# One core, a whole transformer in one launch: both row blocks' norms first, high parts first, and attention products for two heads at a time

## The chip, the cores and the metric

The kernel runs on one core of a Trainium2 chip. Its time is device microseconds, from the first to the last instruction and what lies around them. Engines are TensorE (PE), VectorE (DVE), ScalarE (ACT), GpSimd (POOL) and SyncE (SP), each with an instruction stream of its own that runs in order; semaphores tie them together. Smaller is better.

## The reference, cut to what matters

256 rows of width 1024 pass through seven residual stages, each behind an RMS norm, all in 32-bit floats:

```python
h = h + moba_nsa_mixer(rmsnorm(h, mix_norm[0]), ...)   # "even": 8 full-attention heads, 8 with three gated branches
h = h + sqrelu_mlp(rmsnorm(h, mlp_norm[0]), ...)       # mlp0
h = h + fox_mixer(rmsnorm(h, mix_norm[1]), ...)        # "fox": 16 heads, forget gates
h = h + sqrelu_mlp(rmsnorm(h, mlp_norm[1]), ...)       # mlp1
n = modulate(rmsnorm_2(rmsnorm(h, final_norm), g_ffn1), sh1, sc1); h = h + 0.5 * gt1 * swiglu(n, ...)   # norm gf1, glu0
n = modulate(rmsnorm_2(h, g_mix), sh2, sc2);   h = h + gt2 * hybrid_mixer(n, ...)   # norm gmix, "dil": 8 heads
n = modulate(rmsnorm_2(h, g_ffn2), sh3, sc3);  h = h + 0.5 * gt3 * swiglu(n, ...)   # norm gf2, glu1
out = rmsnorm_2(h, g_final)
```

In the even mixer's second half a head's output is `g0 * o_cmp + g1 * o_slc + g2 * o_win` with `g = sigmoid(...)`, and each `o` is a softmax times values.

## The kernel before

**Products in three parts.** Weights stream in as 173 units of 1 MB through a ring of four buffers `raw`. ACT rounds each to a high part `w_hi`, DVE writes the rest to `w_lo` over `raw`. The rows are split in the same way into `a_hi` and `a_lo`. Each product is three matmuls, high times low, low times high, high times high (`three`, L1532 to L1534). A unit is used when `unit_used` counts it, and SP then loads the unit four further on.

**The rows.** There are two blocks of 128 rows, t = 0 and t = 1. Before each stage a block is normed (`squares`, `root` on ACT, `inverse_root` on DVE), scaled into `tok`, turned on PE by eight transposes (`turn_rows`, L1630, in four chunks of two), rounded by ACT (`turned`, L746, or L748 and L753 where a shift is added: gf1, gmix and gf2) and its low part made by DVE (L1167, or L1154 and L1163). Chunk c of block t is announced by `act_high` and then `act_split`.

**Passages.** A passage is the stretch between two stages. `begin_hidden` (before mlp0, mlp1, glu0, glu1) and `begin_values` (before the values of fox and dil) take the products of block 0, and put the turning of block 1 after three quarters of them:

```python
first_rows(name, u, 1, 0, 0)
turn_rows(name, 1)
first_rows(name, u, 1, 0, 1)
```

Each group of products waits for `act_split`, the last part to be made. The first stage's start is written out by hand in the same manner.

**Mixers.** A mixer walks a list of ticks, written by `plan` from estimated lengths. A tick is a half or a quarter of a weight unit's matmuls, and before them come scores of a head (`tick.s`, L1699 and L1700), turning of probabilities (`tick.t`, L1708) and values times probabilities (`tick.pv`, `products`, L1726). A head goes from PE to DVE (bias and minimum, L1226), ACT (exponential, L827), DVE (reciprocal of the sum, L1244 to L1247), POOL (scaling, L565), PE (turn), and ACT or DVE for even or odd heads (copy into one of six `probT`), and back to PE. `products` treats two heads side by side on 64 columns each of the array; `plan` puts them into a tick when two such pairs are turned. `tick.closed` lists output tiles, which are taken from PSUM one tick later (L838, L1253). The even mixer has a small softmax over compressed keys beside the heads: DVE shifts it in tick km0 2, ACT takes exponentials, DVE weighs it in tick km0 3, and PE turns it in the ticks of `CT_AT`.

## Time and profile before

| what | value |
|---|---|
| median of 3 runs | 1103.0 us (1101.99 to 1103.15) |
| the profiled execution: its time, its span | 1100.71 us, 1098.9 us |
| PE busy | 1075.3 us (98%), 6102 matmuls |
| DVE, ACT, POOL busy | 779.2 us (71%), 662.0 us (60%), 112.8 us (10%) |
| granted PE clock in all 40 slices | 9 (0.9 or more of 2.4 GHz) |
| HBM read | 236.15 MB, 216 GB/s over the span |

PE is in work nearly all the time, so the span is its matmuls one after the other, what lies ahead of the first and behind the last of them, and its waits. "Busy" runs from the start of a matmul to its modelled end, and starts of neighbours lie closer together than that; so the distance between starts is what a matmul costs.

### The profile page before, as it was taken

How to read it: one execution, taken by the hardware profiler on the slowest of the kernel's cores; microseconds unless marked ns; L12 is line 12 of the kernel's file. 1: busy time of each engine (PE TensorE's matmuls, PEld its weight loads, DVE VectorE, ACT ScalarE, POOL GpSimd, SP SyncE). 2: the span in 40 equal slices, each digit the busy share in tenths (PEclk: the TensorE clock that was granted, in tenths of full speed). 3: DMA queues.
4: the chain of work that ended last, by engine and by line, in shares of the span. 5: the costliest groups of instructions: out<-in, count | busy, mean ns of one | idle time of the engine just before them, and what ended most of it. 6: DMA issues, size and time to landing. Idle time of an engine off the chain costs nothing.

```text
span 1098.9 us, 15922 instructions
## 1 busy us (share of the span) xinstructions
PE 1075.3 (98%) x6102; PEld 915.4 (83%) x6102; DVE 779.2 (71%) x1272; ACT 662.0 (60%) x1071; POOL 112.8 (10%) x209
## 2 busy tenths in 40 slices
PE   8999999999999999999999999999999999999997
PEld 7988788888888997888888788888878977888885
DVE  6667667877777776676766778887875766565566
ACT  6667677565576776766565764354475766444443
POOL 1032201010100531020000000101000100000000
PEclk9999999999999999999999999999999999999999
DMA  8842348878764632687778457768545445555551
...
DMA packets 40620, 238.31 MB, mean 217 GB/s; under 512 B 4661, under 2 KB 5845, under 8 KB 17632
## 3 DMA queue, kind: packets, MB, share of 16 engines
...
q8 instruction: 49, 0.80, 0.3%
q10 hardware_dynamic: 720, 0.62, 0.2%
q14 instruction: 27, 0.22, 0.1%
HBM read 236.15 MB, written 1.11 MB: 216 GB/s over the span
## 4 chain that ended last, share of the span: by engine, by line
PE 80%; DVE 9%; ACT 6%; issue 3%; DMA 1%; DVEq 0%; SPq 0%; ACTq 0%
PE bank L1563 21%; PE bank L1532 15%; PE bank L1534 14%; PE bank L1533 14%; PE bank L1564 10%; DVE w_lo L1061 2%; PE bank L1726 1%; PE bank L1708 1%; DMA raw<-in_stream 1%; DVE ada_raw L1296 1%; DVE w_lo L1050 1%; ACT w_hi L683 1%; ACT w_hi L694 1%; PE bank L1700 1%; ACT tok L705 1%
## 5 line engine op out<-in xcount | busy, mean ns | idle before, releaser
L1563 PE MATMUL bank<-a_two,w_hi 128*128 128x512 f32 x1088 | 386.9, 399 | 0.8 <-DVE w_lo L1061 0.8
L1061 DVE TENSOR_TENSOR w_lo<-raw,w_hi 128x2048 fp32r<-128x2048 f32 x122 | 278.5, 2303 | 105.3 <-ACT w_hi L694 105.3
L1564 PE MATMUL bank<-a_two,w_lo 128*128 128x256 f32 x1088 | 305.3, 281 | 0.0
L694 ACT ACTIVATE w_hi<-raw 128x2048 fp32r<-128x2048 f32 x122 | 232.2, 1910 | 63.0 <-DMA raw<-in_stream 62.9
L1563 PEld LDWEIGHTS bank<-a_two,w_hi 128*128 128x128 f32 x1088 | 204.4, 188 | 51.1 <-issue 1.3
L1564 PEld LDWEIGHTS bank<-a_two,w_lo 128*128 128x128 f32 x1088 | 205.5, 189 | 1.7
L1532 PE MATMUL bank<-w_lo,hid_hi 128*128 128x512 f32 x432 | 169.5, 392 | 0.1
L1533 PE MATMUL bank<-w_hi,hid_lo 128*128 128x512 f32 x432 | 168.6, 390 | 0.0
L1534 PE MATMUL bank<-w_hi,hid_hi 128*128 128x512 f32 x432 | 168.4, 390 | 0.0
L866 ACT ACTIVATE cross<-bank 128x256 f32<-128x256 f32 x136 | 51.5, 381 | 187.0 <-PE bank L1564 186.6
L1050 DVE TENSOR_TENSOR w_lo<-raw,w_hi 128x1024 fp32r<-128x1024 f32 x104 | 125.4, 1224 | 25.5 <-ACT w_hi L683 25.0
L683 ACT ACTIVATE w_hi<-raw 128x1024 fp32r<-128x1024 f32 x104 | 106.5, 1050 | 21.2 <-DMA raw<-in_stream 20.9
L1532 PEld LDWEIGHTS bank<-w_lo,hid_hi 128*128 128x128 f32 x432 | 81.1, 188 | 18.9 <-DVE hid_lo L1268 1.0
L1534 PEld LDWEIGHTS bank<-w_hi,hid_hi 128*128 128x128 f32 x432 | 81.1, 188 | 17.8
L1533 PEld LDWEIGHTS bank<-w_hi,hid_lo 128*128 128x128 f32 x432 | 81.1, 188 | 15.2
L1532 PE MATMUL bank<-a_two,w_hi 128*128 128x256 f32 x320 | 93.5, 292 | 0.0
L1534 PE MATMUL bank<-a_two,w_hi 128*128 128x256 f32 x320 | 90.4, 283 | 0.0
L1533 PE MATMUL bank<-a_two,w_lo 128*128 128x256 f32 x320 | 90.4, 282 | 0.0
L1296 DVE CUSTOM_DVE_ANT_0 ada_raw<-ada_raw,silu_row 128x1024 f32<-128x1024 f32 x72 | 84.8, 1219 | 5.2 <-DMA ada_raw<-in_ada 3.5
L1261 DVE TENSOR_TENSOR hid_act<-bank,cross 128x256 f32<-128x256 f32 x96 | 39.1, 420 | 56.5 <-ACT cross L866 56.5
L580 POOL DMA_DIRECT2D ada_raw<-in_ada x72 | 38.1, 530 | 325.9 <-DVE modc L1296 325.9
L1532 PE MATMUL bank<-w_lo,a_two 128*128 128x512 f32 (+1 forms) x160 | 62.1, 388 | 6.1 <-DVE a_two L1167 3.0
...
## 6 DMA issues: line engine op xcount, KB each, us to landing
raw<-in_stream SPq DMA_DIRECT2D x173, 1024.0 KB, 4.9
...
```

The source lines that it names most:

```text
L683: nc.scalar.activation(w_hi[:, u % RING, part_], raw[:, u % RING, part_], ACT.Copy).then_inc(hi_ready, 1)
L694: nc.scalar.activation(w_hi[:, u % RING, :], raw[:, u % RING, :], ACT.Copy).then_inc(hi_ready, 2)
L866: nc.scalar.activation(cross[:, slot, nt, :], ps[bank][:, T:2 * T], ACT.Copy).then_inc(done, 1)
L1050: nc.vector.tensor_tensor(w_lo[:, u % RING, part_], raw[:, u % RING, part_], w_hi[:, u % RING, part_].bitcast(F32), ALU.subtract).then_inc ...
L1061: nc.vector.tensor_tensor(w_lo[:, u % RING, :], raw[:, u % RING, :], w_hi[:, u % RING, :].bitcast(F32), ALU.subtract).then_inc(lo_ready, 2)
L1261: nc.vector.tensor_tensor(to[:, nt * T:(nt + 1) * T], ps[bank][:, 0:T], cross[:, slot, nt, :], ALU.add).then_inc(done, 1)
L1296: nc.vector.tensor_tensor_reduce(part, part, silu_row[:, :], 1.0, 0.0, ALU.mult, ALU.add, modc[:, p:p + 1]).then_inc(ada_done, 1)
L1532: nc.tensor.matmul(dst, l_hi, r_lo, start=start, stop=False)
L1533: nc.tensor.matmul(dst, l_lo, r_hi, start=False, stop=False)
L1534: return nc.tensor.matmul(dst, l_hi, r_hi, start=False, stop=stop)
L1563: nc.tensor.matmul(ps[bank][:, 0:2 * T], wh[:, k, cols_], a_two[:, :, k, :], start=k == 0, stop=False)
L1564: ins = nc.tensor.matmul(ps[bank][:, T:2 * T], wl[:, k, cols_], a_hi[:, k, :], start=False, stop=k == KT - 1)
```

## The change

Five things change.

1. **Start.** The input is loaded in four quarters, on SP's and ACT's queues in turn; half of unit 0 and the table `rpick` move to ACT's queue. DVE squares a half of block 0. Both blocks are normed and scaled before the first weights are split. PE's first products are written out term by term ("h": high times high, "r": high times low weights, "l": low rows), each with its own wait. There are 19 warm-up matmuls where there were 22.
2. **Passages.** `first_rows` and the new `opening` put the products with high rows ahead of those with low rows, and wait for `act_high` and `act_split` apart. Block 1 is turned in two pieces, chunks 0 and 1 an eighth of block 0's products later than before, chunks 2 and 3 another eighth later. DVE's shifts for chunks 1 and 3 no longer come together.
3. **Mixers.** `plan` takes a pair of heads as soon as it is turned, so values times probabilities come for two heads at one time (24 places of one pair, where there were 12 of two). Output tiles are closed one at a tick.
4. **Gates.** The sigmoid is now finished once, in `gates`. DVE's product ahead of each gated head's reciprocal goes, and POOL multiplies by the gate as its second scalar.
5. **Compressed softmax.** Its shift moves to tick km0 3, its exponential to km1 0, its weighing to km1 1, and the first two of its turnings one tick on.

```diff
@@ -43,7 +43,7 @@
-WARM = 22
+WARM = 19
@@ -119,9 +119,9 @@
-            if len(turned) >= 2 and turned[1][0] + lag_pv <= begin:
-                tick.pv += [turned.pop(0)[1], turned.pop(0)[1]]
-                now += 1.3
+            if turned and turned[0][0] + lag_pv <= begin:
+                tick.pv.append(turned.pop(0)[1])
+                now += 0.75
@@ -133,6 +133,9 @@
+    for tick, later, last in reversed(list(zip(ticks, ticks[1:], ticks[2:]))):
+        if len(tick.closed) == 2:
+            later.closed = [tick.closed.pop()] + later.closed
@@ -157,7 +160,7 @@
-CT_AT = [("km1", 0, 1), ("km1", 0, 2), ("qm1", 0, 0), ("qm1", 0, 1)]
+CT_AT = [("km1", 0, 2), ("km1", 0, 3), ("qm1", 0, 0), ("qm1", 0, 1)]
@@ -517,11 +521,9 @@
         def _(sp):
-            sp.dma_start(h[:, 0, :], x[0:P, :]).then_inc(x_landed[0], 16)
-            for part in range(2):
-                part_ = slice(HALF * part, HALF * part + HALF)
-                sp.dma_start(raw[:, 0, part_], stream[0][:, part_]).then_inc(first_landed[part], 16)
-            sp.dma_start(h[:, 1, :], x[P:T, :]).then_inc(x_landed[1], 16)
+            sp.dma_start(h[:, 0, 0:512], x[0:P, 0:512]).then_inc(x_landed[0][0], 16)
+            sp.dma_start(h[:, 1, 0:512], x[P:T, 0:512]).then_inc(x_landed[1][0], 16)
+            sp.dma_start(raw[:, 0, 0:HALF], stream[0][:, 0:HALF]).then_inc(first_landed[0], 16)
@@ -562,7 +564,8 @@
-                        ins = pool.tensor_scalar(p_, p_, wgt[:, 2 * i + t:2 * i + t + 1], 1.0, ALU.mult, ALU.mult)
+                        gate = 1.0 if heads[i][5] is None else gates[:, t, heads[i][5]:heads[i][5] + 1]
+                        ins = pool.tensor_scalar(p_, p_, wgt[:, 2 * i + t:2 * i + t + 1], gate, ALU.mult, ALU.mult)
...
             def mask(c):
@@ -908,22 +910,32 @@
+            act.dma_start(h[:, 0, 512:D], x[0:P, 512:D]).then_inc(x_landed[0][1], 16)
...
+            nc.scalar.activation(stat[:, 10, :], stat[:, 9, :], ACT.Sqrt)
+            act.dma_start(h[:, 1, 512:D], x[P:T, 512:D]).then_inc(x_landed[1][1], 16)
+            act.dma_start(rpick[:, :], rel_pick).then_inc(pick_landed, 16)
+            act.dma_start(raw[:, 0, HALF:UNIT], stream[0][:, HALF:UNIT]).then_inc(first_landed[1], 16)
...
-            squares("mix0", 0)
+            act.wait_ge(x_landed[0][0], 16)
+            nc.scalar.activation(tok[:, 0, 0:512], h[:, 0, 0:512], ACT.Square, scale=1.0 / 32, accum_out=stat[:, 0, 0:1]).then_inc(sumsq, 2)
+            root("mix0", 0)
+            square_half("mix0", 1, 0)
+            square_half("mix0", 1, 1)
+            root("mix0", 1)
...
-            squares("mix0", 1)
...
-            round_half()
...
+            round_half()
@@ -1145,16 +1157,16 @@
-                if shift is not None and chunks[0] == 0:
-                    for c in (1, 3):
-                        dve.wait_ge(bank_turned, m + c + 1)
+                for c in chunks:
+                    if shift is not None and c < 2:
+                        odd = 2 * c + 1
+                        dve.wait_ge(bank_turned, m + odd + 1)
...
-                            dve.wait_ge(act_split, m - 4 + c + 1)
-                        for kt in (2 * c, 2 * c + 1):
-                            ins = nc.vector.tensor_scalar(shifted[:, c, kt % 2, :], ps[TURN_BANKS[name][t][c]][:, (kt % 2) * P:(kt % 2 + 1) * P],
+                            dve.wait_ge(act_split, m - 4 + odd + 1)
+                        for kt in (2 * odd, 2 * odd + 1):
+                            ins = nc.vector.tensor_scalar(shifted[:, odd, kt % 2, :], ps[TURN_BANKS[name][t][odd]][:, (kt % 2) * P:(kt % 2 + 1) * P],
...
-                for c in chunks:
@@ -1238,13 +1250,8 @@
-                        w, d, gate = wgt[:, 2 * i:2 * i + 2], den[:, 2 * i:2 * i + 2], heads[i][5]
...
-                        if gate is None:
-                            nc.vector.reciprocal(w, d).then_inc(weight_ready, 1)
-                        else:
-                            chain(nc.vector.tensor_tensor(w, inv_gates[:, :, gate], d, ALU.mult))
-                            nc.vector.reciprocal(w, w).then_inc(weight_ready, 1)
+                        nc.vector.reciprocal(wgt[:, 2 * i:2 * i + 2], den[:, 2 * i:2 * i + 2]).then_inc(weight_ready, 1)
@@ -1360,20 +1367,23 @@
+            dve.wait_ge(x_landed[0][1], 16)
+            chain(nc.vector.tensor_tensor_reduce(tok[:, 0, 512:D], h[:, 0, 512:D], h[:, 0, 512:D], 1.0 / D, 0.0, ALU.mult, ALU.add,
+                                                 stat[:, 1, 0:1]))
...
+            inverse_root("mix0", 1)
+            scale("mix0", 1)
...
-            inverse_root("mix0", 1)
-            scale("mix0", 1)
...
-            rest_half()
...
+            rest_half()
@@ -1431,14 +1442,14 @@
-                if tick.at("km0", 0, 3):
+                if tick.at("km1", 0, 1):
...
-                    chain(nc.vector.tensor_tensor(w0, inv_gates[:, :, :].rearrange("p t (h b) -> p t h b", b=3)[:, :, :, 0], d0, ALU.mult))
-                    chain(nc.vector.reciprocal(w0, w0))
+                    chain(nc.vector.reciprocal(w0, d0))
+                    chain(nc.vector.tensor_tensor(w0, gates[:, :, :].rearrange("p t (h b) -> p t h b", b=3)[:, :, :, 0], w0, ALU.mult))
@@ -1568,19 +1579,24 @@
-            def first_rows(name, u, j, t, half):
+            def first_rows(name, u, j, t, half, ks=(0, 1)):
...
+                dst = ps[BEGIN_BANKS[t]][:, :]
...
+                pe.wait_ge(act_high, TURN[name] + 4 * t + 2 * j + half + 1)
+                for k in [2 * half + n for n in ks]:
+                    nc.tensor.matmul(dst, a_hi[:, 4 * j + k, ts], wh[:, k, :], start=j == 0 and k == 0, stop=False)
+                    nc.tensor.matmul(dst, a_hi[:, 4 * j + k, ts], wl[:, k, :], start=False, stop=False)
...
-                for k in (2 * half, 2 * half + 1):
-                    ins = three(ps[BEGIN_BANKS[t]][:, :], a_hi[:, 4 * j + k, ts], a_lo[:, 4 * j + k, ts], wh[:, k, :], wl[:, k, :],
-                                j == 0 and k == 0, j == 1 and k == 3)
-                if half == 1 and t == 1:
+                for k in [2 * half + n for n in ks]:
+                    ins = nc.tensor.matmul(dst, a_lo[:, 4 * j + k, ts], wh[:, k, :], start=False, stop=j == 1 and k == 3)
+                if (half, t, ks[-1]) == (1, 1, 1):
...
-                elif (half, j) == (1, 1):
+                elif (half, j, ks[-1]) == (1, 1, 1):
...
             def turn_hidden(name, t):
@@ -1657,21 +1671,47 @@
-                turn_rows(name, 1)
-                first_rows(name, u, 1, 0, 1)
+                first_rows(name, u, 1, 0, 1, (0,))
+                turn_rows(name, 1, (0, 1))
+                first_rows(name, u, 1, 0, 1, (1,))
+                turn_rows(name, 1, (2, 3))
...
-            def begin_values(name, value):
-                value(0, 0)
-                value(0, 1)
-                value(1, 0)
-                turn_rows(name, 1)
-                value(1, 1)
-                for n in range(2):
-                    for part in (2, 3):
-                        value(n, part)
+            def opening(name, phase, j, t, k, terms="hrl", ns=(0, 1), width=D):
+                u = FIRST[phase] + j
+                wh = w_hi[:, u % RING, 0:2 * width].rearrange("p (k c) -> p k c", k=2)
+                wl = w_lo[:, u % RING, 0:2 * width].rearrange("p (k c) -> p k c", k=2)
+                ts = slice(t * P, (t + 1) * P)
+                for term in terms:
+                    if term == "h":
+                        pe.wait_ge(hi_ready, 2 * u + k + 1)
+                        pe.wait_ge(act_high, split_no(name, t, j))
+                    elif term == "r":
+                        wait_weights(u, k)
+                    else:
+                        pe.wait_ge(act_split, split_no(name, t, j))
+                    rows_, weights = (a_lo if term == "l" else a_hi), (wl if term == "r" else wh)
+                    for n in ns:
+                        w = min(512, width - 512 * n)
+                        ins = nc.tensor.matmul(ps[BANK_A[2 * t + n]][:, 0:w], rows_[:, 2 * j + k, ts], weights[:, k, 512 * n:512 * n + w],
+                                               start=(j, k, term) == (0, 0, "h"), stop=False)
+                return ins
+            def begin_values(name, phase):
+                opening(name, phase, 0, 0, 0)
+                opening(name, phase, 0, 0, 1)
+                opening(name, phase, 1, 0, 0)
+                opening(name, phase, 1, 0, 1, ns=(0,))
+                turn_rows(name, 1, (0, 1))
+                opening(name, phase, 1, 0, 1, ns=(1,))
+                turn_rows(name, 1, (2, 3))
+                for j in range(2):
+                    opening(name, phase, j, 1, 0)
+                    opening(name, phase, j, 1, 1).then_inc(unit_used, 1)
...
             def stacked(i):
@@ -1774,18 +1812,24 @@
-            first_value = partial(value_part, "mix0", "v_even", parts=4, width=V1W)
-            first_value(j=0, part=0)
-            first_value(j=0, part=1)
-            pe.wait_ge(pick_landed, 32)
+            pe.wait_ge(pick_landed, 16)
+            pe.wait_ge(relt_landed, 16)
...
+            first_value = partial(opening, "mix0", "v_even", width=V1W)
+            first_value(0, 0, 0, "h")
...
+            first_value(0, 0, 0, "rl")
+            first_value(0, 0, 1, "hlr")
...
-            first_value(j=0, part=2)
-            first_value(j=0, part=3)
-            for part in range(4):
-                first_value(j=1, part=part)
+            first_value(0, 1, 0, "hr")
+            first_value(0, 1, 1, "hr")
+            first_value(0, 1, 0, "l")
+            first_value(0, 1, 1, "l").then_inc(unit_used, 1)
+            for k in range(2):
+                for t in range(TT):
+                    ins = first_value(1, t, k)
+            ins.then_inc(unit_used, 1)
...
             def compressed_heads(n):
```

What the instruction streams say of it, without the numbers of the rows (`[waits ...]` are the semaphores waited for):

PE in the passage to mlp0, from the last products of block 0 ahead of the turning (`par` holds the unit matrix, `tok` the scaled rows, `a_two` both parts of the turned rows). Before:

```order
L1532 MATMUL bank<-w_lo,a_two 128x512
L1533 MATMUL bank<-w_hi,a_two 128x512
L1534 MATMUL bank<-w_hi,a_two 128x512
L1630 MATMUL bank<-par,tok 128x128 [waits rows_scaled_act]
L1630 MATMUL bank<-par,tok 128x128
L1630 MATMUL bank<-par,tok 128x128 [waits rows_scaled_act]
L1630 MATMUL bank<-par,tok 128x128
L1630 MATMUL bank<-par,tok 128x128 [waits rows_scaled_act]
L1630 MATMUL bank<-par,tok 128x128 x3
L1532 MATMUL bank<-w_lo,a_two 128x512 [waits act_split,lo_ready]
L1533 MATMUL bank<-w_hi,a_two 128x512
L1534 MATMUL bank<-w_hi,a_two 128x512
```

After:

```order
L1592 MATMUL bank<-w_hi,a_two 128x512 [waits act_high,lo_ready]
L1593 MATMUL bank<-w_lo,a_two 128x512
L1596 MATMUL bank<-w_hi,a_two 128x512 [waits act_split]
L1644 MATMUL bank<-par,tok 128x128 [waits rows_scaled_act]
L1644 MATMUL bank<-par,tok 128x128
L1644 MATMUL bank<-par,tok 128x128 [waits rows_scaled_act]
L1644 MATMUL bank<-par,tok 128x128
L1592 MATMUL bank<-w_hi,a_two 128x512 [waits act_high,lo_ready]
L1593 MATMUL bank<-w_lo,a_two 128x512
L1596 MATMUL bank<-w_hi,a_two 128x512 [waits act_split]
L1644 MATMUL bank<-par,tok 128x128 [waits rows_scaled_act]
L1644 MATMUL bank<-par,tok 128x128 x3
```

The waits for the third scaled chunk now have three products ahead of them, and one of the remaining products lies between the two pieces; L1592 and L1593 use high rows and L1596 low ones.

PE in the even mixer, around its first values times probabilities (`prob` and `probT` are probabilities and their turned form, `V_all` the values). Before, in tick km0 0:

```order
L1708 MATMUL bank<-par,prob 128x128 x2
L1726 MATMUL bank<-probT,V_all 64x256 [waits probsT_dve,probsT_act]
L1726 MATMUL bank<-probT,V_all 64x256
L1726 MATMUL bank<-probT,V_all 64x128 x2
L1726 MATMUL bank<-probT,V_all 64x256 [waits probsT_dve,probsT_act]
L1726 MATMUL bank<-probT,V_all 64x256
L1726 MATMUL bank<-probT,V_all 64x128 x2
L1532 MATMUL bank<-a_two,w_hi 128x256 [waits lo_ready,feat_taken]
L1533 MATMUL bank<-a_two,w_lo 128x256
L1534 MATMUL bank<-a_two,w_hi 128x256
```

After, in the same tick:

```order
L1748 MATMUL bank<-par,prob 128x128 x2
L1766 MATMUL bank<-probT,V_all 64x256 [waits probsT_dve,probsT_act]
L1766 MATMUL bank<-probT,V_all 64x256
L1766 MATMUL bank<-probT,V_all 64x128 x2
L1543 MATMUL bank<-a_two,w_hi 128x256 [waits lo_ready,feat_taken]
L1544 MATMUL bank<-a_two,w_lo 128x256
L1545 MATMUL bank<-a_two,w_hi 128x256
```

One of two pairs is left there; the other stands two ticks earlier, between turned probabilities and the unit's matmuls, as does every second pair in all three mixers.

DVE in the start (`stat` holds the norm's numbers). Before, from the scaling of block 0:

```order
L1100 TENSOR_SCALAR tok<-h,stat 128x512
L1050 TENSOR_TENSOR w_lo<-raw,w_hi 128x1024 [waits hi_ready]
L1167 SCALAR_TENSOR_TENSOR a_two<-bank,par,a_two 128x128 [waits act_high,norms_landed]
L1167 SCALAR_TENSOR_TENSOR a_two<-bank,par,a_two 128x128
L1050 TENSOR_TENSOR w_lo<-raw,w_hi 128x1024 [waits hi_ready]
L1085 TENSOR_SCALAR stat<-stat 128x1 [waits sumsq]
L1088 TENSOR_SCALAR stat<-stat 128x1 [waits sumsq,mean_ready]
L1090 RECIPROCAL stat<-stat 128x1 [waits root_ready,dve_step]
L1091 SCALAR_TENSOR_TENSOR stat<-stat 128x1 [waits dve_step]
L1092 SCALAR_TENSOR_TENSOR stat<-stat 128x1 [waits dve_step]
```

After, from the same place:

```order
L1112 TENSOR_SCALAR tok<-h,stat 128x512
L1097 TENSOR_SCALAR stat<-stat 128x1 [waits sumsq]
L1100 TENSOR_SCALAR stat<-stat 128x1 [waits sumsq,mean_ready]
L1102 RECIPROCAL stat<-stat 128x1 [waits root_ready,dve_step]
L1103 SCALAR_TENSOR_TENSOR stat<-stat 128x1 [waits dve_step]
L1104 SCALAR_TENSOR_TENSOR stat<-stat 128x1 [waits dve_step]
L1112 TENSOR_SCALAR tok<-h,stat 128x512 [waits inv_ready]
L1112 TENSOR_SCALAR tok<-h,stat 128x512
L1062 TENSOR_TENSOR w_lo<-raw,w_hi 128x1024 [waits hi_ready]
L1179 SCALAR_TENSOR_TENSOR a_two<-bank,par,a_two 128x128 [waits act_high,norms_landed]
L1179 SCALAR_TENSOR_TENSOR a_two<-bank,par,a_two 128x128
```

The five small instructions and the scaling of block 1 have moved ahead of the first two splits of weights.

## Rows read from the trace of the kernel before

**Rows 1.** PE's waits over the whole span: line, released by: us in total, times, longest.

```profile
PE bank L1699 <- DVE low L1226: 3.5, 4, 1.4
...
PE bank L1630 <- ACT tok L761: 3.2, 12, 0.9
...
PE bank L1532 <- DVE a_two L1167: 3.0, 2, 1.8
...
PE bank L1532 <- DVE a_two L1163: 3.0, 3, 1.4
```

**Rows 2.** timeline of the start: start us, us, engine, line, operation [idle before].

```profile
8.28 1.23 DVE L1050 TENSOR_TENSOR w_lo<-raw,w_hi 128x1024 fp32r<-128x1024 f32 x1 [0.21 <-ACT w_hi L683]
...
9.42 0.60 DVE L1167 SCALAR_TENSOR_TENSOR a_two<-bank,par,a_two 128x128 fp32r<-128x128 f32 x2
...
10.00 0.63 ACT L705 ACTIVATE tok<-h 128x512 f32<-128x512 f32 x1
...
10.08 0.50 PE L1532 MATMUL bank<-w_lo,a_two 128*128 128x512 f32 x1 [1.20 <-DVE a_two L1167]
...
12.52 0.88 DVE L1100 TENSOR_SCALAR tok<-h,stat 128x512 f32<-128x512 f32 x2
...
16.59 0.47 PE L1532 MATMUL bank<-w_lo,a_two 128*128 128x512 f32 x1 [1.83 <-DVE a_two L1167]
```

**Rows 3.** two windows: length, busy us (instructions) per engine, PEclk, DMA share, GB/s.

```profile
6.00:9.00 3.00, 2.88 (x25) 2.53 (x23) 2.36 (x7) 1.86 (x5) 0.00 (x0) 1.00 1.04 397
...
20.00:25.00 5.00, 5.00 (x29) 4.34 (x28) 5.00 (x11) 3.59 (x7) 0.00 (x0) 1.00 0.80 262
```

**Rows 4.** timeline around the sixth weight unit and the first heads.

```profile
35.03 1.06 ACT L683 ACTIVATE w_hi<-raw 128x1024 fp32r<-128x1024 f32 x1 [4.69 <-DMA raw<-in_stream]
...
55.37 0.36 PE L1699 MATMUL bank<-k_two,q_two 128*128 128x256 f32 x1 [0.53 <-DVE low L1226]
```

**Rows 5.** timeline of PE in the passage to mlp0: turning of both row blocks.

```profile
143.69 1.04 PE L1630 MATMUL bank<-par,tok 128*128 128x128 f32 x8
...
144.48 0.47 PE L1532 MATMUL bank<-w_lo,q_two 128*128 128x512 f32 x1
...
149.82 0.39 PE L1534 MATMUL bank<-w_hi,a_two 128*128 128x512 f32 x1
...
150.05 0.83 PE L1630 MATMUL bank<-par,tok 128*128 128x128 f32 x4
...
151.47 0.47 PE L1532 MATMUL bank<-w_lo,a_two 128*128 128x512 f32 x1
```

**Rows 6.** timeline of the passage to gf1.

```profile
623.42 0.72 ACT L753 ACTIVATE a_two<-shifted 128x256 fp32r<-128x256 f32 x2
...
624.65 0.47 PE L1532 MATMUL bank<-w_lo,a_two 128*128 128x512 f32 x1 [1.45 <-DVE a_two L1163]
...
629.87 0.84 PE L1630 MATMUL bank<-par,tok 128*128 128x128 f32 x4 [0.86 <-ACT tok L761]
...
631.56 0.72 ACT L753 ACTIVATE a_two<-shifted 128x256 fp32r<-128x256 f32 x2
```

**Rows 7.** timeline of PE, a tick with products of four heads, and one without.

```profile
72.97 0.52 PE L1708 MATMUL bank<-par,prob 128*128 128x128 f32 x3
...
74.87 0.39 PE L1532 MATMUL bank<-a_two,w_hi 128*128 128x256 f32 x1
...
97.93 0.52 PE L1708 MATMUL bank<-par,prob 128*128 128x128 f32 x3
...
98.20 0.36 PE L1532 MATMUL bank<-a_two,w_hi 128*128 128x256 f32 x1
```

**Rows 8.** timeline of PE, its longest waits in the two first mixers.

```profile
86.80 0.36 PE L1699 MATMUL bank<-k_two,q_two 128*128 128x256 f32 x1 [1.42 <-DVE low L1226]
...
91.88 0.52 PE L1708 MATMUL bank<-par,prob 128*128 128x128 f32 x3 [0.60 <-ACT probT L820]
...
415.78 0.36 PE L1699 MATMUL bank<-k_two,q_two 128*128 128x256 f32 x1 [1.07 <-DVE low L1226]
```

39 lines of the change are left out of this document (18 added, 21 removed).

## The prediction

> **What bounds the kernel.** I read the busy shares first: PE 98%, DVE 71%, ACT 60%. The 40 slices show PE at 9 in nearly all of them, and its granted clock is 9 in every one, the upper level of 2.4 GHz, so the clock doesn't enter. The time is therefore PE's matmuls laid end to end, plus its start, tail and waits. The view of PE's waits gives the four groups that the change could touch [rows 1]: four for the high-low score operand from DVE (3.5 us), twelve in the turning of a second row block (3.2), two at the start (3.0) and three at shifted passages (3.0). Only about 12 us stand there, so no edit can bring more than its share of them. Then the timelines: the start [rows 2], where PE waits 1.83 at 16.59 for block 1; DMA's load in two windows [rows 3]; the sixth unit and the first heads [rows 4]; passages [rows 5, 6]; one tick with and one without values times probabilities [rows 7]; the mixers' longest waits [rows 8].
>
> A measurement of this kernel can tell about 0.2%, 2.2 us, from no change. The profiled execution took 1100.71 us, 2.3 below the median of 1103.0; sums are differences, applied to either.
>
> **Start: -1.7 (0 to -3.3).** From the first square of block 1 (10.00) to the end of its scaling (12.52 + 0.88) it takes 3.4 us [rows 2]. These squares move ahead of the weights' rounding. Block 0's scaling ends before 8.07 (DVE is idle 0.21 before 8.28), and what follows its squares takes as long as in block 1, 3.4 less two squares of 0.63, so they end by about 5.9; half of them on DVE makes that some 0.4 earlier. Block 1's squares can follow, but its second half lands at about 6.6: 1 MB of rows at 397 GB/s is 2.6 us [rows 3], and I put the first byte at about 4. Counting a start at 6.4 gives 6.4 + 3.4 = 9.8 for the scaled rows. DVE then has two splits of weights and one pair of low rows, 1.23 + 0.60 + 1.23 = 3.06: it ends at 12.9, and PE's part with block 1, now at 16.59, can begin at about 13.3, 3.3 us earlier. From there PE has 36 matmuls of this unit in a row.
>
> That is the gain at the place; the end gets only a part. The first scores wait for DVE at 55.37 (0.53), and what leads there hangs on unit 6, which landed at 35.03 after ACT had been idle for 4.69 [rows 4]. DMA is full at 6 to 9 (397 GB/s) and has a gap only later (share 0.80 at 20 to 25 [rows 3]). The same bytes come before unit 6 in either kernel, so it moves forward only by what that gap gives: at most (1 - 0.80) x 5 = 1.0 there and some in the stretches beside it. I take 1.7, so that unit 6 lands at about 33.3, PE arrives 3.3 earlier and waits about 0.5 + 1.6 = 2.1 at the first scores. The bound at the one end is that unit 6 doesn't move (0), at the other that the wait stays at 0.53 (-3.3).
>
> The loads of x and unit 0 are shared over two queues. The trace has DMA saturated in that stretch, with one queue doing nearly all of it. A second one can bring the rows' halves earlier but no bytes. The Trainium skill (DMA: Bandwidth & Descriptors, Rules for kernel authors) says that spreading over issuing engines doesn't help bandwidth, and its section on queues, rings and completion order that an engine takes packets of its queues in turn. By that rule half of unit 0 on ACT's queue comes interleaved with the rest instead of behind it; the trace agrees as to the bytes (share 1.04), and has no row on the interleaving.
>
> **Unshifted passages (mlp0, mix1, mlp1): -1.9.** Block 0's turning, all chunks ready, costs 144.48 - 143.69 = 0.79. Block 1's costs 151.47 - 150.05 = 1.42 [rows 5], since PE arrives before ACT has scaled the last chunks; that is the twelve-fold entry of rows 1. The difference is 0.63. Moving the piece later by three matmuls of 0.23 (150.05 - 149.82) and splitting it covers 0.69 for the first two chunks and 1.38 for the rest. So 3 x 0.63. What is late next: the low part of block 1 for PE's products, which have nearly six matmuls less of distance. Those of high rows come first, and so cover it. Bounds: 0 and -1.9.
>
> **Shifted passages (gf1, gmix, gf2): -1.95.** PE waits 1.45 at 624.65 for the low part; with high rows first, about 0.75 of it goes. But PE then meets block 1's turning earlier, at 629.87, where it already waits 0.86 for ACT's scaled rows [rows 6]; this chain of norm doesn't start sooner, so the 0.75 is given back. What stays is that three matmuls, 0.68, stand ahead of the turning instead of behind it, and the rest of the inner wait, against a new wait for the high parts (ACT makes them at 631.56, 0.72 for two; one chunk at a time, now) of about 0.4. Before: turning done at about 631.3, then 30 matmuls of 0.229 = 638.2. After: 632.0 + 24 x 0.229 = 637.5. That is 0.65 to 0.7, three times. Bounds: +0.5 in each (the wait for the high part eats all) and -1.5 (the first wait is kept): +1.5 to -4.5.
>
> **Values times probabilities: +4.6 (+3.5 to +5.5).** A tick's start to its first weight product is 74.87 - 72.97 = 1.90 with two pairs of heads, 98.20 - 97.93 = 0.27 without: 1.63 for a block of two [rows 7]. Streaming: eight matmuls of 128 columns take 1.04 [rows 5] and three 0.52 [rows 7], so 0.104 each; a pair has 256 + 256 + 128 + 128 columns, six such, 0.624, two pairs 1.25. The rest, 0.38, is paid once a block, for going from 128 rows to halves of the array and back. 24 blocks in place of 12: 12 x 0.38 = 4.6. If the halves of the array stream slower than the whole, less of the 1.63 is fixed (bound 0.29 each); if switching costs more when transposes stand ahead, 0.46.
>
> The Trainium skill (TensorEngine Tiling (Array Packing), Tiling Modes) has a rule against this edit: changing the mode drains TensorE. The trace agrees, and the price is the 0.38 above; by the rule the added 12 blocks cost their drains, and without it nothing, which is a rival below.
>
> **Waits absorbed in mixers: -2.5 (-0.5 to -3.5).** The waits of rows 8 stand where DVE or ACT falls behind: 1.42 and 0.60 in the even mixer, 1.07 in fox. The fourth of L1699 is 3.5 - 1.42 - 1.07 - 0.53 = 0.48, in dil [rows 1, 8]. Three edits work on them. A pair of 0.62 + 0.38 = 1.0 us moves into a tick ahead of the scores that wait, and one output tile less is taken by DVE just then: in fox this covers the 1.07, in dil 0.4. In the even mixer the compressed softmax's weighing goes out of km0 into km1, and each gated head has one small DVE operation less (about 0.2 us by the small ones of the norm, an estimate), so 1.42 + 0.60 is about halved: -1.0. It isn't more because the work comes back one tick later, where PE's turning of these probabilities now stands only one tick behind their weighing. POOL's multiplication has a second scalar from memory in place of 1.0; I cost it at nothing, as POOL is 10% busy, and if a head's scaling came 0.3 us later PE has most of a tick of slack.
>
> **Sum.** -1.7 - 1.9 - 1.95 + 4.6 - 2.5 = -3.45. Profiled: 1097.3; median: 1099.5. The tail isn't touched. Three warm-up matmuls less change nothing as long as the first transposes wait for the scaled rows.
>
> **Rivals.**
> (a) Start and mixers give back what they gain: unit 6 lands when it did, and the even mixer's waits only move. 1.7 less and 1.0 to 2.0 less of the absorbed: -0.75 to +0.3, about 1102.5. For it: the saturated DMA [rows 3] and ACT's 4.69 of idle time ahead of unit 6 [rows 4], the plainest sign that data decide there; a longer wait for DVE in the first heads after. Against: the gap at 20 to 25. Chance 0.22.
> (b) Slower: the block of one pair waits for its own probabilities. Before, a block was taken when two pairs were turned, so one pair was old by ticks. Now each goes as soon as one is turned by the plan's estimate. If the copies (ACT for even heads, DVE for odd) end after PE arrives, each of the 24 blocks stalls. Where it is decided: in the tick after the second head's turning, when ACT has a weight rounding of 1.06 [rows 4] or an eviction ahead of the copy. At 0.3 a block this is +7.2: -3.45 + 7.2 = +3.75, 1106.8. It decides from +0.25 a block on (24 x 0.25 = 6 gives +2.5). Against: the waits have no entry for L1726 on ACT or DVE though the newer pair of each block has the same age as now; ACT and DVE are at 60 and 71%. Chance 0.12.
> (c) The start's 3.3 come through, since unit 6 lands early enough, and the passages with a shift keep half of their first wait: -1.6 - 1.1, so -6.15, 1096.9. For it: SP issues loads when units are used, and all of them are used 3 us sooner; against: rows 3. Chance 0.14.
> (d) The drains cost little, as against the rule of the tiles: -8.05, 1095. Against: the 0.38 of rows 7. Chance 0.03.
> (e) That the change doesn't do what it says: the order shows each piece in its new place on PE and DVE, so this I hold below 0.02.
>
> **How the numbers follow.** My forecast, 1099.5, has 0.47, with a range of its own of 1098.0 to 1101.2; the part above 1100.8, about a tenth of it, is within 0.2%. Faster: 0.43 + 0.14 + 0.03 = 0.60. Same: 0.04 + 0.22 and a little of (b) = 0.27. Slower: 0.13. The range leaves out most of (b) above and (d) and the far end of (c) below: 1096.0 to 1104.3.
>
> **What would show it.** Start: block 1's first products at about 13.3; unit 6 landing at 33.3; a wait of about 2.1 before the first scores. Were it 0.5, (c); were it 3.8, (a). Passages: block 1's turning in two pieces with no wait above 0.1 (mlp0); in gf1 a first wait of about 0.7 and a new one of about 0.4 behind the turning. Mixers: 24 blocks, each with 1.0 us from its first matmul to the next product; no waits in them for copies, otherwise (b). Fox's 1.07 gone; the even mixer's two waits at about half, with perhaps a new one in km1. The forecast is wrong if PE's distance sum for blocks grows by less than 3.5 or more than 5.5, or if its waits (some 12 us in rows 1) don't fall by about 6.

## The result, and the profile after

The changed kernel took 1107.41 us (median, 1106.05 to 1108.70), the kernel before 1101.97 in the same series: ratio 1.0041, interval 1.0031 to 1.0052. The two medians differ by 5.4 us, 0.5%; the ratios here and below are those of the record with their 95% intervals, and lie up to 0.0008 beside the quotient of the medians. In a later group of runs the same kernel came to 1.0046 (1.0028 to 1.0064). Forecast were 1099.5 and a range to 1104.3; it went the other way and past the range.

The profiled execution has a span of 1105.8 us, 6.9 more than before. To see where, I took the 5224 matmuls that are products with weights, which both kernels have in nearly the same order, and compared when the n-th of them starts. The table gives the growth of that difference over each stretch, for the changed kernel's profile and for a second profile of it, taken in that later group; the last column is the forecast.

| stretch | first profile | second profile | forecast |
|---|---|---|---|
| start to the first heads (60 us) | +1.4 | +4.6 | -1.7 |
| even mixer | +0.7 | +0.1 | 4.6 - 2.5 = +2.1 for all three |
| passages to mlp0, mix1, mlp1 | -0.1 | 0.0 | -1.9 |
| fox and dil | +0.3 | +0.3 | (above) |
| passage to gf1 | +1.9 | +0.9 | -0.65 |
| passage to gmix | +0.7 | +1.6 | -0.65 |
| passage to gf2 | +1.0 | +2.3 | -0.65 |
| all else | +1.0 | +0.1 | 0 |
| sum | +6.9 | +9.9 | -3.45 |

The mixers came out better than forecast (+1.0 or +0.4 against +2.1). What failed is both parts about waits for other engines, start and passages. Of "all else" in the first profile, 0.9 is one wait for a weight split at 617 us, which the second profile doesn't have and no run here explains. Between two profiles of one kernel places differ by up to 3 us; the granted clock, below, has a part in that.

PE's waits over the whole span, changed kernel (line, released by: us in total, times, longest):

```profile
PE bank L1592 <- DVE w_lo L1062: 5.1, 4, 2.1
PE bank L1818 <- DMA rpick<-in_rel_pick: 1.9, 1, 1.9
PE bank L1700 <- DVE w_lo L1062: 1.8, 2, 1.5
...
PE bank L1644 <- ACT tok L763: 0.6, 3, 0.2
PE bank L1739 <- DVE low L1238: 0.5, 1, 0.5
```

Of the four groups of [rows 1], the scores' fell from 3.5 to 0.5, turning's from 3.2 to 0.6, and those for low rows are gone; for high ones there are new waits, 1.8 in all. In their place stand 6.9 us for low parts of weights (L1592 and L1700 behind `w_lo`), which weren't in the forecast at all, and the start's 1.9 for a table. All that this view lists sums to 18.4 us, where the kernel before has 16.1; the prediction had asked for a fall by about 6.

**Passages.** The timeline of the changed kernel at gf1 (start us, us, engine, line, operation [idle before]):

```profile
630.78 0.61 PE L1596 MATMUL bank<-w_hi,a_two 128*128 128x512 f32 x2
...
632.17 0.16 DVE L1145 SCALAR_TENSOR_TENSOR fin<-fin 128x1 f32<-128x1 f32 x1
632.25 1.22 DVE L1062 TENSOR_TENSOR w_lo<-raw,w_hi 128x1024 fp32r<-128x1024 f32 x1
632.36 1.52 ACT L763 ACTIVATE tok<-h,fin 128x256 f32<-128x256 f32 x3 [0.75 <-DVE fin L1145]
633.52 0.50 PE L1592 MATMUL bank<-w_hi,a_two 128*128 128x512 f32 x1 [2.13 <-DVE w_lo L1062]
...
634.39 1.05 PE L1644 MATMUL bank<-par,tok 128*128 128x128 f32 x4
...
635.09 0.78 PE L1592 MATMUL bank<-w_hi,a_two 128*128 128x512 f32 x1
```

PE is done with three quarters of block 0 at about 631.4. The next eighth, moved ahead of the turning, needs the low part of the last half unit, and DVE makes that in program order behind block 1's norm, 632.25 to 633.47. So PE stands for 2.13 us, while the first scaled rows of block 1, which it could turn, are ready from about 632.9. Before, DVE had the same split in the same place, but the turning stood first on PE, began at 629.87 [rows 6], and covered it:

```profile
629.19 1.22 DVE L1050 TENSOR_TENSOR w_lo<-raw,w_hi 128x1024 fp32r<-128x1024 f32 x1
```

At mlp0 it is the same on a smaller scale:

```profile
151.44 1.22 DVE L1062 TENSOR_TENSOR w_lo<-raw,w_hi 128x1024 fp32r<-128x1024 f32 x1
...
151.66 0.61 PE L1596 MATMUL bank<-w_hi,a_two 128*128 128x512 f32 x2
152.72 0.50 PE L1592 MATMUL bank<-w_hi,a_two 128*128 128x512 f32 x1 [0.44 <-DVE w_lo L1062]
```

The second of the two products of L1596 starts 0.23 after the first, at about 151.89, and the next one 0.83 later where 0.23 is usual. That is 0.60 us lost, of the 0.63 which the moved turning saves.

**Clock.** Five stretches in the view by windows (length, PE busy and instructions, PEclk, DMA share, GB/s), first profile of the changed kernel:

```profile
12.00:16.00 4.00, 3.28 (x13) 0.63 1.03 431
54.00:60.00 6.00, 5.34 (x43) 1.00 1.00 425
634.00:638.00 4.00, 4.00 (x17) 0.57 0.00 0
828.00:832.00 4.00, 3.91 (x21) 1.00 0.25 82
916.00:920.00 4.00, 3.92 (x22) 1.00 0.01 2
```

and second profile:

```profile
54.00:60.00 6.00, 3.77 (x22) 0.76 0.91 378
634.00:638.00 4.00, 2.50 (x14) 1.00 0.00 0
828.00:832.00 4.00, 4.00 (x15) 0.57 0.00 0
916.00:920.00 4.00, 3.02 (x10) 0.66 0.00 0
```

Behind the 2.1 us wait at gf1 the clock is at its lower level, 1.2 GHz, for most of the stretch (the mean of 0.57 takes in its edges) in the first profile and not in the second; behind the waits at the first scores, gmix and gf2 it is the reverse. In passages with a dip the difference grows by 0.9 to 1.3 us more (gf1 1.9 against 0.9, gmix 1.6 against 0.7, gf2 2.3 against 1.0). In the timeline at gf1 it shows as 0.78 for a product in place of 0.39 to 0.50.

**Start.** Chain of waits of the changed kernel (start, us, what):

```profile
28.43 8.02 DMA raw<-in_stream
36.47 1.06 ACT w_hi L685
```

The second half of block 1's rows landed at 10.0, not 6.6, and unit 6 at 36.47, not 33.3; before it was 35.03 [rows 4]. Loads of the first 20 us (KB each, us from issue to landing), and the two queues from 6 to 12 us, while both had work (packets, MB, share):

```profile
raw<-in_stream SPq DMA_DIRECT2D x1, 512.0 KB, 8.2
raw<-in_stream ACTq DMA_DIRECT2D x1, 512.0 KB, 11.6
```

```profile
q1 hardware_dynamic: 250, 1.56, 67.4%
q10 hardware_dynamic: 261, 0.68, 29.7%
```

ACT's queue (q10) moved as many packets as SP's (q1), and less than half of its bytes: its packets had 2.6 KB on average and SP's 6.2. The two halves of unit 0 landed at 9.8 and 14.4, and that holds the start up as well, since ACT, which works in order, had to wait for the rows first and for the second half after that:

```profile
10.01 0.63 ACT L707 ACTIVATE tok<-h 128x512 f32<-128x512 f32 x1 [3.39 <-DMA h<-in_x]
...
11.02 1.04 ACT L685 ACTIVATE w_hi<-raw 128x1024 fp32r<-128x1024 f32 x1
...
14.46 1.06 ACT L685 ACTIVATE w_hi<-raw 128x1024 fp32r<-128x1024 f32 x1 [1.89 <-DMA raw<-in_stream]
...
17.45 0.52 PE L1700 MATMUL bank<-w_hi,a_two 128*128 128x512 f32 x2
```

Before, ACT rounded the first half of the unit at 7.19 and the second soon after:

```profile
9.05 1.06 ACT L683 ACTIVATE w_hi<-raw 128x1024 fp32r<-128x1024 f32 x1
```

The last row of the changed kernel is block 1's first product, which the prediction had at 13.3 and the kernel before at 16.59 [rows 2].

**Blocks.** A tick of the even mixer with one pair, to be read beside [rows 7]:

```profile
68.78 0.52 PE L1748 MATMUL bank<-par,prob 128*128 128x128 f32 x3
69.23 0.87 PE L1766 MATMUL bank<-probT,V_all 128*64 128x256 f32 x8
70.03 0.39 PE L1543 MATMUL bank<-a_two,w_hi 128*128 128x256 f32 x1
```

From 68.78 to 70.03 are 1.25 us, less the 0.27 without a block [rows 7] 0.98; two of them are 1.96 where a block of two cost 1.63. So one more block costs 0.33, twelve cost 4.0 (forecast 4.6).

### The profile page after: what moved, and what is told of

It is laid out like the page before. It is cut to its first block, busy times and chain, and to the rows that moved or that the text cites. A ratio compares the mean times of both kernels' runs of the same rounds, so it can differ in the third digit from the quotient of the medians.

```text
span 1105.8 us, 15921 instructions
## 1 busy us (share of the span) xinstructions
PE 1079.9 (98%) x6096; PEld 918.7 (83%) x6096; DVE 779.9 (71%) x1259; ACT 662.5 (60%) x1069; POOL 112.6 (10%) x208
## 4 chain that ended last, share of the span: by engine, by line
PE 76%; DVE 11%; ACT 7%; issue 4%; DMA 2%; ACTq 0%; DVEq 0%
PE bank L1574 19%; PE bank L1543 13%; PE bank L1544 12%; PE bank L1545 12%; PE bank L1575 10%; DVE w_lo L1062 2%; DVE w_lo L1073 2%; ACT w_hi L696 2%; PE bank L1766 2%; PE bank L1700 2%; DMA raw<-in_stream 2%; PE bank L1748 1%; DVE ada_raw L1303 1%; ACT w_hi L685 1%; ACT tok L707 1%
## 5 line engine op out<-in xcount | busy, mean ns | idle before, releaser
L1574 PEld LDWEIGHTS bank<-a_two,w_hi 128*128 128x128 f32 x1088 | 204.4, 188 | 51.2 <-issue 1.6
L1543 PEld LDWEIGHTS bank<-a_two,w_hi 128*128 128x128 f32 x320 | 61.1, 191 | 2.9 <-issue 2.8
```

What stands on the lines that cost most here:

```text
L1543: nc.tensor.matmul(dst, l_hi, r_lo, start=start, stop=False)
L1574: nc.tensor.matmul(ps[bank][:, 0:2 * T], wh[:, k, cols_], a_two[:, :, k, :], start=k == 0, stop=False)
```

## The experiments

All are timed in 5 rounds, in groups on one chip with the kernel before beside them; ratios are to that. By the width of the intervals, two kernels of different groups differ clearly only from about 0.0015 on. Where a cut of a diff leaves lines out, `...` stands for them.

### What each part costs

**The list of ticks alone**, on the kernel before:

```diff
-            if len(turned) >= 2 and turned[1][0] + lag_pv <= begin:
-                tick.pv += [turned.pop(0)[1], turned.pop(0)[1]]
...
+            if turned and turned[0][0] + lag_pv <= begin:
+                tick.pv.append(turned.pop(0)[1])
...
+            later.closed = [tick.closed.pop()] + later.closed
```

> The kernel before, with the new list of ticks alone (24 blocks of one pair of heads for 12 of two, output tiles closed one at a tick). By my count 12 x 0.38 us more for the blocks, and of the waits for scores and copies 1.42 + 0.60 + 1.07 + 0.48 some 3 us absorbed: +1.0 to +2.0 us over before. Rival 1, the blocks wait for their own probabilities: +4 or more, with PE waits at the values-times-probabilities line. Rival 2, extra blocks are nearly free: -2 to -3.

Ratio 1.0012 (1.0000 to 1.0025), +1.3 us, as the count has it. PE's waits have no entry at the values-times-probabilities line, so rival 1 (my rival (b)) is out. The even mixer has a longer wait instead, at the turning of probabilities (2.7, where the kernel before has 1.0 at that line):

```profile
PE bank L1711 <- ACT probT L823: 2.7, 2, 2.1
```

**Mixers' edits all together**, and **gates and compressed softmax alone**, both on the kernel before:

```diff
-                            chain(nc.vector.tensor_tensor(w, inv_gates[:, :, gate], d, ALU.mult))
...
+                        ins = pool.tensor_scalar(p_, p_, wgt[:, 2 * i + t:2 * i + t + 1], gate, ALU.mult, ALU.mult)
...
-                if tick.at("km0", 0, 3):
+                if tick.at("km1", 0, 1):
```

> The kernel before with all the edits of the mixers (list of ticks, gates, compressed softmax) and none of start and passages. Against the list alone (ratio 1.0012), gates and softmax should be worth the 1.5 to 2 us by which the even mixer lost less in the changed kernel than in that one: ratio 0.999 to 1.000, PE's wait of 2.1 us for ACT's turned probabilities gone. Rival: they only move waits, ratio as the list alone.

> The kernel before with the gates and the compressed softmax alone (no new list, start or passages). My theory: they take most of the 1.42 and 0.60 us waits of the even mixer, -1 to -2 us, ratio 0.998 to 0.999. Rival: no effect without the new list (ratio 0.9995 to 1.0005).

Ratios 1.0012 (1.0002 to 1.0023) and 0.9999 (0.9988 to 1.0011). Gates and softmax alone are worth nothing that can be told, and with the list neither (1.0012 with them, 1.0012 without); I had expected 1 to 2 us. PE's waits there show why: the scores still wait 2.0 in three places, and the turning of the small softmax, one tick behind its weighing, waits 1.4 where it didn't before.

```profile
PE bank L1705 <- ACT probT L821: 2.0, 2, 1.9
PE bank L1696 <- DVE low L1227: 2.0, 3, 1.1
PE bank L1856 <- DVE pc L1441: 1.4, 1, 1.4
```

With the list these fall to 1.1, 0.3 and 0.6, 3.4 us less, and the list still costs 1.4 us net (1.0012 less 0.9999): 4.0 for blocks, most of it earned back by shorter waits.

**The changed kernel with the old list:** the first edit undone.

> The changed kernel with the old list of ticks (12 blocks of two pairs of heads). If the extra blocks' 0.38 us is what the list costs and the gates and the compressed softmax have already taken the waits away, this is 2 to 4 us faster than the changed kernel (ratio to before 1.001 to 1.003 instead of 1.004). If the list absorbs as much as it costs, within 1 us of it.

Ratio 1.0027 (1.0014 to 1.0040) against 1.0041 and 1.0046: 1.5 to 2 us less, with intervals that overlap. Three comparisons give 1.3, 1.4 and about 1.8 for the list.

**Old list and old passages as well**, so that start, gates and softmax are left:

```diff
-                first_rows(name, u, 1, 0, 1, (0,))
-                turn_rows(name, 1, (0, 1))
-                first_rows(name, u, 1, 0, 1, (1,))
-                turn_rows(name, 1, (2, 3))
+                turn_rows(name, 1)
+                first_rows(name, u, 1, 0, 1)
...
-                pe.wait_ge(act_high, TURN[name] + 4 * t + 2 * j + half + 1)
+                pe.wait_ge(act_split, TURN[name] + 4 * t + 2 * j + half + 1)
```

> The changed kernel with passages as before (turning in one piece, waits for low parts, DVE's shifts together) and the old list of ticks: start, gates and compressed softmax are left of the change. If the start loses by its loads and its clock: +1 to +2 us over before (gates and softmax alone had ratio 0.9999), ratio 1.001 to 1.002. If only passages lose: ratio 0.9985 to 1.000.

Ratio 0.9997 (0.9986 to 1.0009). The start as changed neither gains nor loses at the end; passages are the 1.0027 - 0.9997 = 0.0030, 3.3 us, that is left. **The yardstick** of that group:

> The changed kernel once more, on the chip of these runs, as the yardstick: ratio 1.004 to 1.005, mean granted clock about 0.994.

Ratio 1.0046, mean clock over its runs 0.9934; its profile is the second one above.

### Passages

**Turning in one piece, on PE alone**, at gf1, gmix and gf2 (the same order in `begin_values` for gmix):

```diff
+                if name in ("gf1", "gf2"):
+                    turn_rows(name, 1)
+                    first_rows(name, u, 1, 0, 1)
```

> The changed kernel, with PE's turning of block 1 back in one piece after three quarters of block 0's products, in the three shifted passages alone. Theory: the eighth of products that was moved ahead of the turning needs a weight split which DVE makes behind block 1's norm; PE waits for it (2.1 us at gf1, 1.5 at gmix), so this kernel is 3.5 to 5 us faster than the changed one, about 1103. Rival: DVE's new order of shifts delays the chain; then nothing changes here (within 1 us of 1107.4).

The trace agrees: PE's products gain and lose nothing in the three passages (at most 0.1 us each, against +1.9, +0.7 and +1.0), and the wait for `w_lo` at gf1 is one for scaled rows:

```profile
632.11 1.22 DVE L1062 TENSOR_TENSOR w_lo<-raw,w_hi 128x1024 fp32r<-128x1024 f32 x1
632.23 1.52 ACT L763 ACTIVATE tok<-h,fin 128x256 f32<-128x256 f32 x3 [0.75 <-DVE fin L1145]
632.79 0.84 PE L1644 MATMUL bank<-par,tok 128*128 128x128 f32 x4 [1.52 <-ACT tok L763]
```

The runs' times say less: ratio 1.0025 (1.0012 to 1.0037), 1.8 to 2.3 us less than the changed kernel and not 3.5 to 5. Its runs lie from 1103.1 to 1107.3, the fastest with a mean clock of 0.999, the others with 0.994 to 0.997. The wait of 1.5 us that is left here can bring the dip too: a combination below with the same order has it at gf1 and gf2. That this is what the other runs of this kernel lost is not shown.

**DVE's shifts together again**, as before, on the changed kernel:

```diff
-                    if shift is not None and c < 2:
-                        odd = 2 * c + 1
...
+                if shift is not None and chunks[0] == 0:
+                    for c in (1, 3):
```

> The changed kernel, with DVE's shifts for chunks 1 and 3 together again, as before. Theory (weight split behind the norm on DVE): no gain, 0 to +1.5 us on 1107.4, since DVE then also waits for PE's second piece. Rival (the new order of shifts costs the time): 3 us or more faster.

Ratio 1.0049 (1.0030 to 1.0068). No gain: the order of shifts isn't the cause.

**DVE's split ahead of the norm's end:**

```diff
+                    rest_half()
                     both_norms_root(1)
                 else:
+                    rest_half()
                     inverse_root(name, 1)
-                rest_half()
```

> The changed kernel, with DVE's split of the last weights of a passage ahead of block 1's norm's root (in gf1 ahead of the last root) and not behind it, in all passages. Theory: the waits for that split (0.44 us at mlp0, 2.1 at gf1, 1.5 at gmix) vanish or shrink by a microsecond, 0.4 us gained in each unshifted passage, and 1 to 2 in the shifted ones, total 3 us or more faster than the changed kernel (ratio 1.001 to 1.002). Rival: the chain of the norm is delayed by the split's 1.22 us and PE waits as long for block 1's scaled rows (ratio 1.004).

Ratio 1.0069 (1.0055 to 1.0083): slower still, beyond the rival's 1.004 too, so my remedy was wrong. In the passage to mlp0 DVE, with the split first, waits 0.71 us for ACT's rounding, and the reciprocal behind the split comes 1.5 us later than in the changed kernel (after the 3.05 us by which the two are apart ahead of the passage is taken off):

```profile
153.71 1.23 DVE L1062 TENSOR_TENSOR w_lo<-raw,w_hi 128x1024 fp32r<-128x1024 f32 x1 [0.71 <-ACT w_hi L685]
...
155.43 0.16 DVE L1102 RECIPROCAL stat<-stat 128x1 f32<-128x1 f32 x1 [0.18 <-ACT stat L721]
...
156.64 0.84 PE L1645 MATMUL bank<-par,tok 128*128 128x128 f32 x4 [0.62 <-ACT tok L763]
```

PE needs both, the split and the scaled rows, and DVE makes one behind the other. With the norm first, PE's moved products wait for the split; with the split first, its turning waits for the rows.

### The clock's share

**Waits filled** in the three shifted passages of the changed kernel, with unused matmuls into a free bank (5 at gmix):

```diff
+                if name in ("gf1", "gf2"):
+                    for _n in range(7):
+                        nc.tensor.matmul(ps[BEGIN_BANKS[1]][:, :], a_hi[:, 0, 0:P], w_hi[:, u % RING, 0:512], start=True, stop=True)
```

> The changed kernel, with 7 matmuls (gf1, gf2) or 5 (gmix) of 128x512 that compute nothing used, into block 1's bank, just ahead of the eighth of products that waits for DVE's weight split. They take 1.6 and 1.15 us of waits of 2.1, 1.5 and 2.1. In the changed kernel's profile the granted clock behind the wait at gf1 is 0.56 and 0.59 for 4 us (1.2 GHz), and its mean over the runs is 0.9942 where before has 0.9975. Theory (the wait costs itself and again as much through the clock): granted clock 1.0 behind both waits, mean clock 0.996 or more, 1.5 to 3 us faster than the changed kernel (ratio about 1.002). Rival (the clock's dip is a byproduct and not what costs): no difference, ratio 1.004.

**Start filled as well**, 30 + 14 small matmuls, then 16 + 7:

```diff
+            for _n in range(16):
+                nc.tensor.matmul(ps[6][:, 0:P], probT[:, 0, 0:P], probT[:, 0, 0:P], start=True, stop=True)
             pe.wait_ge(pick_landed, 16)
```

> As the kernel with filled waits in the shifted passages, and with 30 + 14 small unused matmuls in the start's two waits (for the picked table and for the first rounded rows). The changed kernel's clock there is 0.75, 0.50 and 0.89 in the stretches from 12 to 18 us. Theory: clock 1.0 there, another 0.5 to 1.5 us faster than the passages' filling alone, mean clock 0.998. Rival: PE waits for data there anyway, and nothing is gained at the end, since the first scores wait for DVE.

> The changed kernel with the unused matmuls in the shifted passages, and at the start 16 + 7 small ones in place of 30 + 14, since one takes 0.114 us and not half of it: 1.8 and 0.8 us in waits of 1.9 and 1.0. Theory (the dip of the clock at the start costs about 1 us, and fillers of the right length bring it back): clock 1.0 from 12 to 18 us, 0.5 to 1.5 us faster than the kernel with filled passages, 1.5 to 3 us faster than the changed kernel. Rival (the first scores wait for DVE, so nothing of the start reaches the end): as the kernel with filled passages.

Ratios of the three: 1.0045 (1.0032 to 1.0057), 1.0078 (1.0064 to 1.0091) and 1.0035 (1.0024 to 1.0046). My sizes for the small ones were wrong twice: the trace counts two instructions for each, so one takes 0.23 us. The 44 took some 10 us for waits of 3, which is why that kernel is slowest, and says nothing of the clock. The first kernel, with passages filled and the start as it was, is no faster than the changed one (1.0041, 1.0046), though its clock is 1.00 in all three passages. The 23 overshot at the start, by 2 us (last row against 12.72 in the changed kernel):

```profile
8.51 3.74 PE L1822 MATMUL bank<-probT 128*128 128x128 f32 x32
...
13.13 1.83 PE L1829 MATMUL bank<-probT 128*128 128x128 f32 x14
14.71 0.61 PE L1703 MATMUL bank<-w_hi,a_two 128*128 128x512 f32 x2
```

At 22 us 0.4 of these 2.0 were left against the changed kernel's first profile and nothing against its second; both of those have a dip from 13 to 16 us, this one has none. The clock is full in all the stretches shown above:

```profile
12.00:16.00 4.00, 4.00 (x30) 1.00 1.00 422
634.00:638.00 4.00, 3.92 (x21) 1.00 0.00 0
828.00:832.00 4.00, 3.91 (x20) 1.00 0.40 128
916.00:920.00 4.00, 3.92 (x20) 1.00 0.01 2
```

and the mean clock over its runs 0.9985 against 0.9934 for the yardstick of its group. Against that one the time fell by 0.0011, 1.2 us, with intervals that overlap. Passages without dips still cost 0.9, 0.7 and 1.0 us in this trace, as they do without fillers where no dip follows. So by this experiment the dips are a minor part, about 1 us of 5 and not shown beyond noise, and the waits themselves the larger one. The 1.5 to 3 us I expected of fillers didn't come. The runs' own clocks point to more: among the 29 runs of the kernel before in this group a mean clock lower by 0.001 goes with 0.85 us (a straight line through them), among the 8 of the changed kernel with 0.81, and the two kernels are 0.004 apart, which would be 3.3 us. But a longer wait can cause both, the lost time and the dip behind it, so that is no price of the dips.

### The start's loads

**Block 1's second half and unit 0's on SP's queue**, the rest as changed:

```diff
+            sp.dma_start(h[:, 1, 512:D], x[P:T, 512:D]).then_inc(x_landed[1][1], 16)
             sp.dma_start(raw[:, 0, 0:HALF], stream[0][:, 0:HALF]).then_inc(first_landed[0], 16)
+            sp.dma_start(raw[:, 0, HALF:UNIT], stream[0][:, HALF:UNIT]).then_inc(first_landed[1], 16)
...
-            act.dma_start(h[:, 1, 512:D], x[P:T, 512:D]).then_inc(x_landed[1][1], 16)
...
-            act.dma_start(raw[:, 0, HALF:UNIT], stream[0][:, HALF:UNIT]).then_inc(first_landed[1], 16)
```

> The changed kernel, with the second half of block 1's rows and the second half of unit 0 loaded by SP's queue, in front of units 1 to 3, in place of ACT's. Theory (a queue with packets of 2 KB gets a small share beside one with 8 KB): block 1's second half lands by about 7 instead of 10.0, the second half of unit 0 by about 9 instead of 14.4, PE's products with block 1 begin 2 to 3 us earlier, and the end comes 1.5 to 3 us earlier than the changed kernel. Rival (bytes set it, whatever the queue): under 0.7 us of difference.

Ratio 1.0028 (1.0017 to 1.0039), 1.5 to 2 us less than with the loads as changed. Its timeline has block 1's second half by 7.8 where it was 10.0, and the first products 1.8 earlier:

```profile
7.77 0.63 ACT L709 ACTIVATE tok<-h 128x512 f32<-128x512 f32 x1 [1.25 <-DMA h<-in_x]
...
10.95 0.60 PE L1700 MATMUL bank<-w_hi,a_two 128*128 128x512 f32 x2 [1.47 <-ACT a_two L750]
```

At 22 us PE is 3.4 us ahead of the changed kernel and 2.6 ahead of the one before, close to the 3.3 that the prediction had for the place. And as it also had, the end gets only a part: unit 6 landed at 35.05, no earlier than before, and PE waits 2.2 at the first scores. The edit changes two things at once, the queue and so the order in which the loads come; packets of another size on ACT's queue were not tried.

### Combinations

**Old list, these loads, turning in one piece at the shifted passages, and DVE's split first at the others**, then the same with 5 fillers each ahead of the turning at gf1 and gf2:

> A combination: the changed kernel with the old list of ticks, the rows and unit 0 loaded by SP's queue as in the loads' experiment, block 1 turned in one piece after three quarters in the shifted passages, and in the unshifted passages DVE splitting the weights ahead of block 1's norm, so that PE doesn't wait for them. From the parts: start and even mixer -1, unshifted passages 3 x -0.4, shifted 0, mixers -1 to -2: 3 to 5 us faster than before, 1098 to 1100 (ratio 0.9955 to 0.9975). If only the sign of the passages is right: ratio 0.998 to 1.000.

> The combination of the earlier experiment (ratio 1.0002), with 5 unused matmuls of 128x512 ahead of block 1's turning at gf1 and gf2, where its profile shows a wait of 1.5 us and the clock at 0.50 and 0.75 for 4 us, each costing 1.4 us. Theory: both are gone, 1.5 to 3 us faster than that combination, ratio 0.9975 to 0.999. Rival: ratio 1.000 to 1.0005.

Ratios 1.0002 (0.9992 to 1.0012) and 0.9996 (0.9987 to 1.0005), both above what I mainly expected. The early split costs 0.4 us in each unshifted passage by the trace, and in the first one gf1 and gf2 cost 1.4 each, with the clock at its lower level, and gmix nothing at full clock; fillers took that away at gf1 and gf2, and gmix, unfilled, had the lower clock and cost 1.5. With the turning in one piece, then, a dip costs 1.4 to 1.5 us where it comes, and the passage without it nothing.

**Only what had helped**, that is the kernel of start, gates and softmax with the loads mended:

> As the last one, with block 1's second half and unit 0's second half on SP's queue. Theory: the start is 3.4 us earlier at its own place, of which about 1.5 reach the end because unit 6 and the first scores come only 0.8 us earlier; 1 to 2.5 us faster than before, ratio 0.9975 to 0.999. Rival (nothing of it reaches the end): ratio 1.000.

1100.15 us against 1102.64, ratio 0.9971 (0.9958 to 0.9985): it beats both kernels, by 2.5 to 3 us the one before, a little more than the 1 to 2.5 expected. Its chain of waits:

```profile
24.81 9.24 DMA raw<-in_stream
34.07 1.06 ACT w_hi L684
```

Unit 6 was asked for 2.9 us earlier than before (24.81 against 27.67 in that view) and landed 1.0 earlier, after 9.24 us where it took 7.3. DMA's share is 1.01 from 20 to 34 us, where it was 0.92: the gap is filled, and it gave the 1.0 us that the prediction had worked out for it, not the 1.7 that it then took. PE, 2.9 us ahead at 22, waits 1.9 at the first scores, is 1.0 ahead there and 1.7 at the end of the even mixer, and keeps 1.6 to the end of the profiled execution.

## Why the prediction was wrong, by its steps

**Start, -1.7.** Two steps failed. "Its second half lands at about 6.6" took bytes in the order of need; it was on ACT's queue, in turn with 4 and 8 KB packets of SP's, and landed at 10.0. The same queue brought unit 0's second half at 14.4, to which the prediction gave no price, and block 1's first products came at 17.45, not 13.3. I had cited the Trainium skill (DMA: Bandwidth & Descriptors, Queues, rings and completion order) for it that an engine takes packets of its queues in turn, and drew nothing from it for the rows; the trace agrees with it (250 and 261 packets from 6 to 12 us). Then unit 6 at about 33.3: it landed at 36.47. With the loads mended the place gained 2.9 (forecast 3.3), unit 6 came at 34.07 to 35.05, and 1.6 us reached the end in the profile of the best kernel, 2.5 to 3 in its times: mechanism right for those loads, not for these. Measured for the start as changed: nothing (0.9997 with gates and softmax, 0.9999 for those alone).

**Unshifted passages, -1.9.** Failed at "What is late next: the low part of block 1". Next was the low part of the last half unit: 0.60 is lost there at mlp0 where 0.63 was to be saved; measured for the three, 0.0. That the 0.63 were the twelve waits of [rows 1] was misread too: in the kernel before each of these three passages has one of them, of 0.2 us, and 2.7 of the 3.2 lie in the shifted ones. The rest of the 0.63 is in the distances between the turning's matmuls.

**Shifted passages, -1.95.** The chain of the norm didn't start sooner, as forecast, and the first wait did shrink to 0.8. Failed at "three matmuls, 0.68, stand ahead of the turning instead of behind it" as a gain: they wait 2.1, 1.5 and 2.1 us for that split, so +2.6 us without dips of the clock, and +1.0 and +2.2 more in the two profiles that have one and two of them. The trace of before had the row, the split of 1.22 us behind the norm at 629.19; I asked what the moved products need of rows, not of weights.

**Blocks, +4.6.** Right; 12 x 0.33 = 4.0.

**Waits absorbed, -2.5.** Right in sum (2.2 to 2.7: 4.0 less the list's 1.3 to 1.8), though it is the list that earns it, not gates and softmax (0 by themselves against the 1.0 I gave them); the sum came out by two misses that cancel.

**Rivals.** (a) came nearest on the start, where data decide; but its +0.3 at most doesn't reach 5.4. (b), my slower one, was at the wrong place: no block waits for its copy. None had the split of weights. The parts sum to 0 for the start, 1.4 for the list, 3.3 for passages: 4.7, against 4.5 to 5.1 measured by ratio (5.4 by the medians).

Open is how often a wait is followed by the lower clock, and whether what it costs in the median is next to nothing or up to 3 us: fillers changed the mean clock clearly, and the time within the noise.
